# A two-block transformer kernel: an 8-row transpose and three expert columns set ahead of TensorE's first up loop

## The reference, cut to what matters

```python
def block(xb):                                  # 128 tokens
    q = (xb @ w_query).reshape(PEER_TOKEN_BLOCK, PEER_HEADS, 2, D_KEY // 2)
    s = jnp.einsum('thpc,pkc->thpk', q, sub_keys)
    s1, i1 = lax.top_k(s[:, :, 0], PEER_TOPK)
    s2, i2 = lax.top_k(s[:, :, 1], PEER_TOPK)
    ...                                         # 16 best pairs of each head: experts e, scores sc
    g = jax.nn.softmax(sc, axis=-1)
    u = expert_u[e]
    act = jax.nn.gelu(jnp.einsum('td,thkd->thk', xb, u))
    return jnp.einsum('thk,thkd->td', (g * act), expert_v[e])
```

## Time and profile before

| | |
|---|---|
| timed runs | 1286.74, 1284.17, 1283.83 us, median 1284.17 |
| profiled execution | 1291.12 us, of it span 1289.3 us |
| mean granted clock of TensorE | 0.992 |
| TensorE matmul busy | 1252.8 us, 97% of the span |
| VectorE, ScalarE, GpSimd busy | 707.1 (55%), 677.1 (53%), 650.4 us (50%) |
| HBM read | 215.50 MB |
| up columns of the first loop | 176.0 to 354.2 us |
| gating stage | 364.6 to 596.3 us |
| down columns | 597.2 to 947.3 us |

### The profile page before, as it was taken

One profiled execution on the slowest core, in us unless ns is written; L12 is line 12 of the kernel. 1 busy time (PEld: TensorE's weight loads), 2 busy tenths in 40 slices (PEclk: granted clock), 3 DMA queues, 4 the chain that ended last, 5 costly groups with the idle time before them and its releaser, 6 DMA issues.

```text
span 1289.3 us, 26634 instructions
## 1 busy us (share of the span) xinstructions
PE 1252.8 (97%) x9857; PEld 1199.6 (93%) x9857; DVE 707.1 (55%) x1494; ACT 677.1 (53%) x1203; POOL 650.4 (50%) x285
## 2 busy tenths in 40 slices
PE   7998999999999999999999999999999999899996
PEld 5887999999989999999999999999999988699885
DVE  2453059980156667775666666666656742446424
ACT  4585444444566655555444555444564564446553
POOL 6756868888866666664000000000038666577654
PEclk9998999999999999999999999999999999899998
DMA  6735545555534444445666656666675433454432
GB/s 214 260 115 180 180 139 187 183 191 180 186 140 145 139 144 148 147 138 191 195 194 193 192 191 192 194 195 195 194 238 174 148 133 114 163 166 144 137 129 98
DMA packets 59300, 218.70 MB, mean 170 GB/s; under 512 B 6688, under 2 KB 6856, under 8 KB 58848
## 3 DMA queue, kind: packets, MB, share of 16 engines
q1 hardware_dynamic: 56592, 206.07, 48.6%
q0 software_dynamic: 1792, 8.95, 1.9%
q10 hardware_dynamic: 848, 2.75, 0.6%
HBM read 215.50 MB, written 4.21 MB: 170 GB/s over the span
## 4 chain that ended last, share of the span: by engine, by line
PE 93%; DVE 2%; POOL 2%; ACT 2%; issue 1%; DMA 0%; POOLq 0%; DVEq 0%; ACTq 0%
PE W L499 28%; PE A L499 27%; PE W L761 4%; PE A L543 4%; PE A L523 4%; PE A L550 4%; PE A L545 4%; PE A L524 4%; PE A L528 4%; POOL ringl L427 2%; PE A L663 1%; PE W L925 1%; PE A L658 1%; PE A L660 1%; PE W L577 1%
## 5 line engine op out<-in xcount | busy, mean ns | idle before, releaser
L427 POOL TENSOR_TENSOR ringl<-ring,ringh 128x1024 fp32r<-128x1024 f32 x137 | 338.0, 2486 | 151.2 <-ACT ringh L996 144.2
L457 POOL TENSOR_TENSOR ringl<-ring,ringh 128x1024 fp32r<-128x1024 f32 x126 | 302.4, 2400 | 116.7 <-ACT ringh L1154 78.7
L499 PE MATMUL W<-XTh,ringh 128*128 128x256 f32 x1024 | 292.1, 285 | 0.1
L499 PE MATMUL W<-XTl,ringh 128*128 128x256 f32 x1024 | 286.7, 280 | 0.0
L499 PE MATMUL W<-XTh,ringl 128*128 128x256 f32 x1024 | 286.6, 280 | 0.0
L499 PE MATMUL A<-Hh,ringh 128*128 128x256 f32 x1024 | 282.8, 276 | 0.0
L499 PE MATMUL A<-Hl,ringh 128*128 128x256 f32 x1024 | 282.6, 276 | 0.0
L499 PE MATMUL A<-Hh,ringl 128*128 128x256 f32 x1024 | 282.6, 276 | 0.0
L996 ACT ACTIVATE ringh<-ring 128x1024 fp32r<-128x1024 f32 x135 | 141.7, 1057 | 141.3 <-PE A L550 51.5
L1154 ACT ACTIVATE ringh<-ring 128x1024 fp32r<-128x1024 f32 x189 | 197.5, 1045 | 0.4 <-DMA ring<-exp_v 0.4
L499 PEld LDWEIGHTS W<-XTh,ringh 128*128 128x128 f32 x1024 | 195.5, 191 | 0.3 <-ACTq L1099 0.3
(11 more groups left out here) (262 smaller groups left out, 2054.0 us busy)
## 6 DMA issues: line engine op xcount, KB each, us to landing
ring<-exp_u SPq DMA_DIRECT2D x128, 512.0 KB, 3.2
ring<-exp_v SPq DMA_DIRECT2D x128, 512.0 KB, 4.2
ring<-w SPq DMA_DIRECT2D x72, 512.0 KB, 3.2
ring<-w_out SPq DMA_DIRECT2D x24, 512.0 KB, 3.2
ring<-w_in SPq DMA_DIRECT2D x20, 512.0 KB, 3.5
ring<-w_query SPq DMA_DIRECT2D x16, 512.0 KB, 3.2
skewed<-scratch POOLq DMA_DIRECT2D x1, 2048.0 KB, 11.1
H<-lng POOLq DMA_DIRECT2D x2, 1024.0 KB, 7.5
```

The source lines that it names most:

```text
L427: pool.tensor_tensor(ringl[:, slot, :], ring[:, slot, :], ringh[:, slot, :].bitcast(F32), ALU.subtract)\
L457: pool.tensor_tensor(ringl[:, slot, :], ring[:, slot, :], ringh[:, slot, :].bitcast(F32), ALU.subtract)\
L499: last = pe.matmul(dst, stationary[a], moving[b], start=start and n == 0, stop=stop and n == 2, skip_group_check=True)
```

## The change

Ahead of the loop TensorE waits for the load of GF and for what the first column needs, transposes the 8 x 128 tile GF into the first 8 columns of bank 0 of `W4`, and runs the first three up columns. The loop then makes 20 turns in place of 21, with its counts shifted by three units. The transposed values are read by nobody, since the first column overwrites the bank; the later transpose of GF stays.

```diff
-            def ahead(i, s):
-                pe.wait_ge(lo_done, SLOTS * i + (U_PEER1 + s + 1))
-                pe.wait_ge(u_gelu, SLOTS * i + (s + 1))
+            def ahead(i, s, first=0):
+                pe.wait_ge(lo_done, SLOTS * i + (U_PEER1 + SLOTS * first + s + 1))
+                pe.wait_ge(u_gelu, SLOTS * i + (SLOTS * first + s + 1))
                 up((U_PEER1 + s) % SLOTS, s)
 
-            with pe.Fori(0, U_AHEAD // SLOTS - 1) as i:
+            pe.wait_ge(end_gain, 16)
+            pe.wait_ge(lo_done, U_PEER1 + 1)
+            pe.wait_ge(u_gelu, 1)
+            pe.transpose(W4[:, 0, 0:KC], GF[:], ident[0:KC, 0:KC])
+            for s in range(SLOTS):
+                ahead(0, s)
+            with pe.Fori(0, U_AHEAD // SLOTS - 2) as i:
                 for s in range(SLOTS):
-                    ahead(i, s)
+                    ahead(i, s, 1)
```

## The result

The changed kernel took 1289.57 us (median of 8 runs, 1282.29 to 1296.13), the kernel before 1283.61 us beside it (8 runs, 1281.59 to 1286.74): a ratio of 1.0046, 95% interval 1.0028 to 1.0064. I had forecast 1277.6 us, so even the sign was wrong on that chip. In later batches the ratio was 1.0028 (1.0012 to 1.0044), 1.0010 (0.9978 to 1.0043) and 1.0007 (0.9995 to 1.0018). The profiled execution took 1290.35 us, against 1291.12 before: the two profiles alone would have said that nothing happened.

What follows compares the result with a forecast made beforehand. TensorE, busy 97% of the span, was taken to bound the kernel. Faster up loop -6.7 us and added transpose +0.15 gave -6.55, so the median of 1284.17 would become 1277.6 us, range 1276.2 to 1285.3.

Steps and rivals of the forecast that it cites:

- What bounds the kernel: Whole kernel: TensorE, busy 97% of the span and 93% of the chain, sets the end by its own pace.
- The pace of the loop, removed: Up loop: with the 8-row transpose ahead, 178.19 us becomes 171.5 us; -6.7 us, bounds 0 and -6.9.
- 3 of 3: 8-row transposes in first layer, second layer and ahead of the down loop: products behind each last 276 ns, the fast pace.
- my nearest row: Start of the down columns: same shape and engine, three waits and an 8-row transpose ahead, taken to show the fast pace.
- The bound of 0: Up loop: the gain is 0 if the pace stays slow despite the transpose.
- From the profile to the median: Whole kernel: profiled execution is 6.95 us over the median; the same is subtracted after the change, giving 1277.6 us.
- runs without the profiler are fast already: Rival, up loop: recording tips the pace or adds the rest, so the timed median stays, 1284.3 us; chance 0.10.
- each restart draws its pace anew: Rival, down loop: the shifted program could make 123 fast down columns slow, +13.0 us, 1290.6 us in all; chance 0.07.
- The transpose and the waits: Ahead of the up loop: added transpose costs +0.15 us, bounds +0.1 and +0.4; the three added waits cost 0.
- a restart by a change of height: Behind the 8-row transpose: 0.23 us to the second matmul agrees with the skill's engine drain at a tiling mode change.
- Three columns ahead of the loop: Up loop entry: columns moved out, 20 turns for 21, cost 0; lower bound 0, upper +0.4 us if loop code came late.
- Nothing late next: Up loop and picks: POOL and ACT fit under 2.72 us a column; picks' margin of 1.5 us shrinks by 0.3 and holds.

Runs made afterwards that it cites:

- the second burst kernel: Kernel before plus 72 bursts of 24 products ahead of the up columns, with idleness, met waits and 8-row transposes tried between; 1504.04 us, repeated 1506.15 us.
- the first burst kernel: Kernel before plus a loop of 6 turns of 12 bursts of 24 products, behind different odd instructions, ahead of the up loop; 1509.66 us, repeated 1507.93 us.
- the last experiment: Kernel before, three up columns moved ahead, odd instruction behind first up and first down column: 64-row products 1283.38 us, 128-row transposes 1294.49 us.

## Why the prediction was wrong, step by step

*What bounds the kernel* was right. So was the worth of the pace: 6.7 us forecast, 6.70 measured between the two paces. The fast loop takes 171.49 us from start to start (171.5 forecast).

*The pace of the loop, removed*, is the step that failed. I took 3 of 3 starts behind 8-row transposes as a property of that transpose. They were starts of one execution, and two of them the same place in two layers. The changed kernel's loop was slow behind it in two profiles of four, and the down loop, my nearest row, was slow behind it in the kernel with the 64-row product ahead. The second profile of the unaltered kernel was enough to see it. There the start in the second layer, one of the three, is slow (1128.4 to 1130.1 us, answers to the third line of the earlier trace rows):
```profile
L545 PE MATMUL A<-XTl,ringh 128*128 128x256 f32 x6 | 1.5, 281 | 0.0
```
What the runs showed in its place is a transpose that mostly turns the pace over. It did so 6 of 6 from either side in the second burst kernel. Over the 15 profiles it did so in 15 of 15 down loops, and a pair of them did so in the second layer in 15 of 15 (slow and then fast in the first profile alone, fast and then slow in the 14 others), and in the first layer in 10 (slow and then fast; in the other 5 it was fast on both sides). In the profile that I read, all three starts stood behind slow products. At the up loop that is not the whole of it. In the kernel before the up loop had the pace of the query groups ahead of it in 3 profiles of 3. In the six profiles with the 8-row transpose ahead of the up loop and nothing else odd, the query groups were fast each time, and the loop was slow in three and fast in three. What decides there stays open. The bound of 0 was the value that the first profile gave.

*From the profile to the median* failed with it, and explains the sign. I subtracted 6.95 us from both, as if the profiled execution were an ordinary one plus an overhead. It was an execution with the slow loop (and slow query groups), while most runs of the kernel before had the fast one: 7 of its 8 on that chip were below 1286. There was nothing left to gain in them. The median of the changed kernel was high there because 6 of its 8 runs lay above 1286. The rival "runs without the profiler are fast already" named this state (1284.3 us; the last two batches gave 1283.52 and 1283.71), but put it down to the recording. The rival "each restart draws its pace anew" had the mechanism, and I gave it 0.07 because I looked for it only in the down loop.

*The transpose and the waits*: +0.15 forecast for the one and 0 for the others, together 0.33 - 0.10 = 0.22 us before rounding (last key product to first up product 603 ns against 385 in the profiles of both). Within the bounds. The half with the transpose alone had 882 ns, 0.50 us more than before, so the halves don't add up to the whole; why is not shown. I had read the 0.23 us behind the transpose as agreeing with a restart by a change of height. The rows don't single it out: it stands behind the full-height products with the keys too. In the first burst kernel the first product behind an odd instruction was 201 to 203 ns ahead of the second where the odd one had 128 rows and 128 columns, and 222 where it had 8 or 64 rows. The height shows on the other side: from the last product of a burst to the odd instruction were 206 to 212 ns with 8 or 64 rows, and 113 to 122 with 128.

*Three columns ahead of the loop*: no cost in the loop. The profile of that half alone had 694 ns between the last key product and the first up product, 0.31 us more than before; within the upper bound of 0.4.

*Nothing late next* was right, shown by the fourth profile of the changed kernel, whose loop was fast: POOL's wait fell to 16.4 / 52 = 0.32 us (0.31 forecast), and the picks' last step ended at 343.27, 1.2 us before their transposes (1.2 forecast). Its groups of 200 to 340 us, and its timelines of DVE and TensorE:
```profile
L457 POOL TENSOR_TENSOR ringl<-ring,ringh 128x1024 fp32r<-128x1024 f32 x52 | 124.9, 2402 | 16.4 <-ACT ringh L1114 16.4
```
```profile
340.92 2.35 DVE L1512 TENSOR_TENSOR H<-H,gs 128x128 f32<-128x128 f32 x1
...
344.50 0.71 PE L752 MATMUL A<-cst,H 128*128 128x128 f32 x5
```

Is the changed kernel slower, then? By about 0.2 us for the transpose, as the rows show. Beyond that, 17 of its 44 runs lay above 1286: 6 of 8, 6 of 12, 4 of 12, 1 of 12, against 1 of 8, 0 of 47, 16 of 35 and 1 of 35 of the kernel before beside it. The second pair is no accident of counting, yet the third and fourth went the other way or nowhere, and the fourth was on the chip of the second. So the program alone doesn't fix the odds; whether chip or hour joins in, these batches can't tell. What in an execution draws the pace of the up loop stays open: in two profiles the start is alike to 0.01 us and the pace is not. That the change in general makes the kernel 0.46% slower is not shown.

## What to carry to other kernels

A profile is one execution. Before a pattern in it is made the ground of a change, see whether it comes again in a second profile of the same kernel, and whether the profiled time is where the median is: a profile 6.95 us above the median, in a kernel with a stretch that could be 6.7 us shorter, said that most runs were without it. "Three of three" counts for little when all three are of one execution, and all the less when what stood ahead was alike too: the products ahead of each were slow, and a start that turns the pace over then looks like one that makes it fast. And where a program has such draws, count its runs on either side of a cut that profiles bear out, in more than one batch and on more than one chip, before a shift of 0.3 to 0.5% is put down to an edit.

## What the runs showed of the hardware

- A stream of products of one shape (128x128 weights, 256 columns, one weight load each), without idleness and at the full granted clock, has two stable paces, 113.3 and 117.8 ns. It is settled in the first six products or fewer and then held over up to 2952 of them. Which of the two it is differs between executions of the same program. The Trainium skill, "TensorE: Matmul & The Clock Gate", section "Wait — 56ns, not 53.3ns?", has one spacing for warm matmuls, 109.2 ns here, an estimate by its formula; the traces show two, both longer.
- In a dense stream the kind of odd instruction between the products decided the pace, alike in two executions of the first burst kernel (12 lines of 12): slow behind a 128x128 transpose, fast behind 64-row and 128-row products of 128 columns, and slow behind a 512-column product, which here stood behind fast bursts only. Yet in the last experiment the up loop of one profile had the other pace behind the 64-row product, in a stream as dense.
- The 8-row transpose turned the pace over in a dense stream, 6 of 6 from either side, in both executions of the second burst kernel. Ahead of the down loop it did so behind 0.50 to 0.59 us of idleness, in 15 profiles of 15, and in the second layer in 15 of 15. It isn't a law: in the first layer the products were fast on both sides in 5 profiles of 15, and one line, behind idleness, of the second burst kernel was slow in one execution and fast in the other.
